# GpSimd starts the copies of the attention caches when x has landed instead of when the third group of weights has

## What is computed

```python
def trunk_layer(x, start_pos, conv_buf, pool_buf, k_buf, v_buf, ...):
    h = rms_norm(x, norm_g)
    proj = jnp.einsum('btd,de->bte', h, w_in)     # 1024 -> 3200 columns
    ...                                           # convolution group, pooling group, q, k, v, gates
    kk = jnp.concatenate([k_buf, k], axis=1)
    vv = jnp.concatenate([v_buf, v], axis=1)
    o = dilated_attention(q, kk, vv, k_buf.shape[1])
    ...
    new_k = kk[:, -n_keep:]                       # the cache, moved on by one token
    new_v = vv[:, -n_keep:]
    y = jnp.einsum('bte,ed->btd', jnp.concatenate([ya, yb, yc], axis=-1), w_out)
    return x + y, new_conv, new_pool, new_k, new_v
```

## Time and profile before

| | |
|---|---|
| median of 3 runs | 440.1 us (437.45 to 445.49) |
| the profiled execution | 439.78 us, of which the span of its instructions is 438.0 us |
| busy share of the span | PE 79%, DVE 53%, ACT 24%, POOL 9% |
| moved by DMA | 158.06 MB in 47301 packets, mean 361 GB/s |
| HBM | read 154.90 MB, written 104.42 MB |

### The profile page before, as it was taken

One profiled execution on the slowest core, in us unless ns is written; L12 is line 12 of the kernel. 1 busy time (PEld: TensorE's weight loads), 2 busy tenths in 40 slices (PEclk: granted clock), 3 DMA queues, 4 the chain that ended last, 5 costly groups with the idle time before them and its releaser, 6 DMA issues.

```text
span 438.0 us, 4497 instructions
## 1 busy us (share of the span) xinstructions
PE 347.8 (79%) x1552; PEld 269.3 (61%) x1552; DVE 232.1 (53%) x522; ACT 103.2 (24%) x243; POOL 38.4 (9%) x70
## 2 busy tenths in 40 slices
PE   1799999947897999997999998498979999960000
PEld 1688888835675656886888887367755568840000
DVE  0626997998677643104278979985865421100000
ACT  4101145223342131102011533143321401130000
POOL 0014101100101011010011001110100111110000
PEclk9999999996999899999999999969989999995555
DMA  8999999999999999999999999999999999999941
GB/s 296 360 368 298 375 365 395 414 389 409 418 414 390 336 342 368 424 417 390 414 394 405 393 415 349 380 407 418 412 364 326 329 329 326 332 333 379 330 182 49
DMA packets 47301, 158.06 MB, mean 361 GB/s; under 512 B 3861, under 2 KB 16351, under 8 KB 46703
## 3 DMA queue, kind: packets, MB, share of 16 engines
q0 software_dynamic: 22592, 100.62, 62.7%
q1 hardware_dynamic: 15508, 33.85, 21.2%
q10 hardware_dynamic: 9178, 23.31, 14.2%
HBM read 154.90 MB, written 104.42 MB: 592 GB/s over the span
## 4 chain that ended last, share of the span: by engine, by line
PE 58%; DVE 16%; DMA 8%; ACT 3%; issue 2%; SPq 1%; ACTq 0%; DVEq 0%
PE pj L543 28%; PE pj L682 13%; DMA kv<-in_cache_v_win 7%; PE psc L614 6%; DVE kv L1058 4%; DVE ssc L1061 4%; DVE yc L1118 3%; PE ptr L469 2%; PE ps L491 2%; DMA cst<-in_const 1%; SPq L373 1%; PE psc L469 1%; PE ps L665 1%; PE prt L555 1%; PE ps L553 1%
## 5 line engine op out<-in xcount | busy, mean ns | idle before, releaser
L543 PE MATMUL pj<-hT,w 128*128 128x264 f32 x800 | 188.8, 394 | 3.0 <-DVE hT L980 3.0
L543 PEld LDWEIGHTS pj<-hT,w 128*128 128x128 f32 x800 | 152.9, 194 | 32.6 <-issue 7.0
L1118 DVE SCALAR_TENSOR_TENSOR yc<-u_ext,par,yc 128x256 f32<-128x256 f32 x180 | 76.2, 480 | 2.8 <-DVE u_smp L1008 0.6
L682 PE MATMUL pj<-mix,w 128*128 128x264 f32 x256 | 59.3, 386 | 0.0
L682 PEld LDWEIGHTS pj<-mix,w 128*128 128x128 f32 x256 | 48.5, 190 | 8.2
L1188 DVE TENSOR_TENSOR xT<-xT,pj 128x264 f32<-128x264 f32 x16 | 6.9, 429 | 53.6 <-PE pj L682 53.6
L461 POOL DMA_DIRECT2D out<-in_cache_v_win x32 | 18.6, 581 | 186.4 <-issue 186.4
L461 POOL DMA_DIRECT2D out<-in_cache_k_win x32 | 18.6, 584 | 160.5 <-issue 129.4
L614 PE MATMUL psc<-kv,spm 128*48 128x384 f32 x80 | 27.5, 496 | 0.4 <-DMA kv<-in_cache_v_win 0.4
L803 ACT ACTIVATE ex<-pj 128x264 f32<-128x264 f32 x22 | 8.6, 390 | 75.1 <-PE pj L543 60.9
L909 ACT ACTIVATE hT<-xT 128x264 f32<-128x264 f32 x16 | 6.8, 423 | 66.1 <-DVE xT L1188 66.1
(11 more groups left out here) (169 smaller groups left out, 331.5 us busy)
## 6 DMA issues: line engine op xcount, KB each, us to landing
out<-in_cache_k_win POOLq DMA_DIRECT2D x32, 1512.0 KB, 72.1
out<-in_cache_v_win POOLq DMA_DIRECT2D x32, 1512.0 KB, 68.9
w<-in_w_out ACTq DMA_DIRECT2D x2, 4096.0 KB, 28.9
w<-in_w_in ACTq DMA_DIRECT2D x1, 4608.0 KB, 29.0
kv<-in_cache_k_win SPq DMA_DIRECT2D x32, 144.0 KB, 28.4
w<-in_w_in ACTq DMA_DIRECT2D x3, 1536.0 KB, 27.5
kv<-in_cache_v_win SPq DMA_DIRECT2D x32, 144.0 KB, 20.7
w<-in_w_in SPq DMA_DIRECT2D x1, 4608.0 KB, 28.5
```

The costliest lines, as they stand in the source:

```text
L543: last = nc.tensor.matmul(pj[n % RING][:, 0:T], wbuf[buf][:, k, col:col + P], hT[:, k, :], start=(k == 0), stop=(k == KD - 1))
L682: last = nc.tensor.matmul(pj[n % RING][:, 0:T], w1[:, k, m * P:(m + 1) * P], mix[:, k, :], start=(k == 0), stop=(k == KD - 1))
L1118: last = V.scalar_tensor_tensor(out=yc[:, t, 0:SEQ], in0=x_w, scalar=par[:, ROW_CW + w * CT + t:ROW_CW + w * CT + t + 1], in1=yc[:, t, 0:S ...
```

## The change

GpSimd's first wait is for x (`x_in` at 32, both parts landed) and no longer for the weights of `a_gate`. No instruction is added, removed or put elsewhere on any engine.

```diff
             for name in START:
                 pool.sem_inc(S[name], 1)
 
-            pool.wait_ge(S["a_gate_in"], 16)
+            pool.wait_ge(x_in, 32)
             for l in reversed(range(DEPTH)):
                 for i, (kind, s, h) in enumerate(HALVES):
                     cache, out = (ins["cache_k_win"], o_k_s) if kind == "k" else (ins["cache_v_win"], o_v_s)
```

## The result

The changed kernel took 425.2 us (median of 4 runs, 423.52 to 430.63) beside 440.7 us for the kernel before, measured next to it (437.45 to 445.49): a ratio of 0.966, 95% interval 0.958 to 0.974. Ratios here leave out executions over 1.5% above the fastest of their kernel, so they can differ from the quotient of the medians. The two medians of the changed kernel lie 1 us apart; those of the kernel before went from 434.5 to 440.7. The gain is 10.6 to 15.5 us by the medians and 8.7 to 15.0 by the ratios: it is clear of zero both times, and clear of 2% only the first time. The forecast was 435.2 with a range of 430 to 442.

The account below looks back on a forecast made before the run. It took the DMA traffic and its rate, with copies ending last, as the bound: 438.0 - 4.9 - 0.7 + 0.7 = 433.1 us of span, 434.9 with the 1.78 us around it, so 435.2; range 430 to 442.

Parts of the forecast that it names:

- What bounds the kernel: Whole span: DMA traffic with its copies, not compute, done 45.8 us earlier; engines full except at the end, leaving the rate.
- (a): Start of the copies: first issue at 7.6 us, 24.0 us before 31.59; 7 us to first data, so data from 14.6.
- (b): Price of a copy packet: 215 ns alone, 174 ns beside loads, so 41 ns of one engine saved each.
- (c): Copy packets moved from time alone to shared time: 1900 to 2160, taken as 1900, for 4.9 us less.
- (d): Loads beside copies: first q, k and v weights 8% cheaper per KB, 0.7 us less; nothing at q1's small packets.
- (e): Fall in rate when copies begin, 255 GB/s in 31 to 36 us: moved, not removed; cost 0, bounds -2.7 and +2.7.
- (f): Engines that end late, 418 to 438 us: lag unchanged or 1.5 us more with shared time; middle taken, +0.7.
- Rival C: Late engines' lag grows with three queues for 24 us more, adding 7.3 us: slower, 441.8 to 444.5; chance 0.08 (440.5 to 446).
- (g): Compute waits longer for weights and keys, ending at 400 to 410 us, not 392; cost nothing, hidden behind the copies.
- Rival D: Compute becomes the bound, needing over 40 us of delay; time then above 440; chance 0.02 together with the rest.
- Rival A: Early start counts in full, copies ending 24 us sooner: 416; full form, under 428, chance 0.04; mild form 431.2, 0.14.
- the additions of the forecast: From span to time: 1.78 us around the span, and 0.3 us by which the profiled execution lay under the median.

Follow-up runs that it names:

- start_kin: Changed kernel with GpSimd's first wait for the landing of the first key gathers, not x; first copy at 53.4 us: 443.6 us, ratio 1.021 to the kernel before.
- start_now: Changed kernel with no wait before GpSimd's copies, which start at once, first copy at 1.8 us: 418.8 us, ratio 0.964 to the kernel before.

## Why the prediction was wrong

*What bounds the kernel* was right: copies end last, compute has slack (45.8 us before, 15.2 after), the engines have no hole to fill, and only the rate can give something.

*(a)* The start was right to 0.6 us. The delay from issue to data, taken as 7 us, was too long: in the changed kernel 192 copy packets have passed by 16 us (below), and at the steady rate of a shared stretch (937 in 20 us) that is 4 us of traffic, so data from about 12 us. Counted in stretches of 1 us, the first copy packets pass at 12 to 13 us, 4 to 5 us after the issue; in the two traces of before it is 5 to 6 us, with gathers in the other queues, and in `start_kin`, with nothing in them, about 1.

```profile
q1 hardware_dynamic: 766, 2.36, 74.7%
q0 software_dynamic: 192, 0.88, 26.9%
```

*(b) and (c)*, the copy packets beside loads: 4.9 us less was forecast. GpSimd's queue took 274.6 and 275.7 us in the two traces of before (63.8% of 432.2) and 270.3, 270.3 and 269.5 in the three after: 5.1 less. The count was right too. The loads are over by 330 us before and by 340 to 345 in the changed kernel, and until then 15977 and 15760 copy packets have passed before, and 17763, 17725 and 17551 after: 1800 more in company, with 1900 forecast.

*(d)*, the loads, is the term that failed with (e): 0.7 us forecast, with nothing to gain at SyncE's small packets. Measured: ScalarE's queue fell from a mean of 62.7 to 59.3 us and SyncE's from 93.5 to 91.0, together 6.0 us before rounding. I had priced a load packet alone from 24 to 31 us, before the gathers came, and taken it for all loads.

*(e)*, the fall of the rate, was given the wrong cause. I saw 255 GB/s begin where the copies begin, called it a cost of their start, and moved it along at no gain, -2.7 us at best. `start_kin` shows the fall with no copies at all: gathers alone run at 239 to 250 GB/s, and slow the weights beside them as well. With copies beside them the stretches of gathers run at 358 to 416 (50 to 90 us of the changed kernel). The early start gives the gathers that company from their first packet on, where before they had it only from 38 to 40 us. The 1.4 MB gained in 31 to 40 us are worth 4.4 us at the end, where (e) had 0. This is the same gain as that of the queues above, seen by stretch, and is not to be added to it.

*(f)*, the late engines, was put at +0.7 with Rival C behind it. Neither showed: the idle time at the end is 6.0 to 15.4 us before and 7.4 to 8.8 after. The forecast started from the trace with 15.4, so in that pair of traces 6.6 us of the 14.3 us of span are idle time at the end, beside 9.0 us of packet time. That scatter may well be why the measured gain lies between 10.6 and 15.5 us around the 11.1 us of packet time; two traces of before don't show it. No size under it can be settled by one trace.

*(g)*, compute: the first projection at 22.64 us is 3.9 later (1 to 2 forecast), since the first weights landed at 20.5 us and not at 17 or 18; the wait for `a_gate` 2.2 us (4 to 5), the first `sscore` at 91.57 us after a wait of 6.4 (85 to 90, 3 to 8), the end at 408.5 (400 to 410). All of it is hidden, as forecast. (In its working "57 ns" is a slip; the 0.42 us of a turn holds the 64.) Rival D was no danger here; in `start_now` its cover was down to 4.8 us.

*The rivals.* The time fell under 428, where only Rival A's full form stood, with 0.04. That form, 24 us, was wrong too, since it had all 24 us come back; but its argument, that a full DMA share is no full rate, was the right one. I weighed it against 383 to 390 GB/s before the start of the copies, and not against the 255 just after. The profile's sign for it was on record as well: copies that end much before 430 mean that the fall is gone. With (d) at 6.0 and (b, c) at 5.1 the sum would have been 438.0 - 11.1 = 426.9 of span, and 429.0 by the additions of the forecast. That is still 3.8 us over the 425.2 measured; the rest is of the size of the scatter in (f), and no run assigns it.

*The limit.* The about 358 GB/s for a core's HBM traffic that the Trainium skill gives ("DMA: Bandwidth & Descriptors", section "Specifications") did not bound this kernel, which runs on one core: it moved 411 to 421 GB/s over the 32 us from 8 to 40.

## What to carry to other kernels

Where DMA traffic is the bound, compare GB/s and the time of a packet by stretch and not the engines' busy share: at a share of 1.0 the rate here was anything from 238 to 421 GB/s. Put transfers that nobody waits for beside the slow kinds of loads, from the first microsecond, as long as the compute that they delay stays hidden. A forecast that starts from one trace has to carry the scatter of that trace's end, 6 to 15 us of idle time here. When a rate falls where something starts, look for what else starts there: one run with the suspected cause held back tells them apart.

## What the runs showed of the hardware

Gathers of 144 and 192 KB, each over 16 partitions and from one cache, ran at 239 to 250 GB/s without copies (weights beside them until some 40 us) with the DMA share at 1.02 to 1.06; copies from HBM to HBM ran at 326 to 330 alone, in one queue or two; gathers beside copies, with or without weights, ran at 358 to 416. Farther reads and spread writes raised the gathers alone to 270 and 277 GB/s in one stretch of 4 us, both together to 302, and brought the keys at most 1 us earlier; what holds them was not found. A transfer whose source has 4 as its slowest dimension ran on about 4 of the 16 engines; with all gathers in that form the kernel took some 190 to 210 us longer.
